# GpSimd instead of SyncE issues the loads of the values v in the recurrence of an RWKV-7 layer

## The reference

```
def step(state, inp):
    r_t, w_t, k_t, v_t, kk_t, a_t = inp
    sa = einsum('bhvk,bhk->bhv', state, kk_t)
    state = (state * w_t[:, :, None, :] - sa[..., None] * (kk_t * a_t)[:, :, None, :]
             + v_t[..., None] * k_t[:, :, None, :])
    return state, einsum('bhvk,bhk->bhv', state, r_t)
```

## Time and profile before

| | |
|---|---|
| three executions | 1603.55, 1608.61, 1597.57 us (median 1603.55) |
| profiled execution | 1597.2 us, its span 1595.4 us |
| busy share of the span | TensorE 91%, VectorE 32%, ScalarE 15%, GpSimd 12% |
| TensorE's granted clock over the span | 0.984 of full speed |
| recurrence | about 269 us (first fill of unit 0) to 537 us (first product of the next stage) |
| transfers issued by SyncE (queue q1) | 180192 packets, 479.31 MB, 78.4% of 16 engines |
| transfers issued by GpSimd (queue q0) | 5792 packets, 19.88 MB, 3.6% of 16 engines |
| four times eight `UV` loads | SyncE, 128 KB each, 5.2 us to landing (median) |

### The profile page before, as it was taken

How to read it: one execution, slowest core, us unless ns; L and a number is a source line. 1 busy time by engine, 2 the same in 40 slices (tenths; PEclk the granted TensorE clock), 3 DMA queues, 4 the chain that set the end, 5 groups by cost and what they waited for, 6 DMA issues and landing times.

```text
span 1595.4 us, 26196 instructions
## 1 busy us (share of the span) xinstructions
PE 1453.7 (91%) x11376; PEld 727.9 (46%) x11376; DVE 509.8 (32%) x712; ACT 239.9 (15%) x478; POOL 184.2 (12%) x349
## 2 busy tenths in 40 slices
PE   8999999988887895999989989989989989989977
PEld 6344455888887553434324324324324324324322
DVE  6666534666664564001101101101101101101103
ACT  3333321222212121100000000000000000000002
POOL 1323503433333210000000000000000000000000
PEclk9999999999999997899999999999999999999999
DMA  9245577766765635599999999999999999999994
GB/s 302 66 158 184 185 264 162 180 132 138 145 117 145 265 146 211 207 426 424 424 425 426 424 426 426 425 425 426 426 424 427 425 425 428 423 426 427 421 425 187
DMA packets 186071, 500.47 MB, mean 314 GB/s; under 512 B 125905, under 2 KB 135249, under 8 KB 153217
## 3 DMA queue, kind: packets, MB, share of 16 engines
q1 hardware_dynamic: 180192, 479.31, 78.4%
q0 software_dynamic: 5792, 19.88, 3.6%
HBM read 470.83 MB, written 28.33 MB: 313 GB/s over the span
## 4 chain that ended last, share of the span: by engine, by line
PE 32%; DMA 24%; DVE 2%; issue 1%; ACT 1%; DVEq 0%; SPq 0%
DMA ring<-in_exp_w_up 24%; PE pD L1555 14%; PE pG L1516 6%; PE pU L1536 6%; PE pX L1504 4%; PE pG L1536 3%; DVE res L1664 1%; DVE hid L1682 1%; PE pX L1543 1%; ACT hidT L1625 0%; DVE res L1700 0%; ACT xin L1608 0%; PE pX L1572 0%; ACT xin L1640 0%; ACT L1643 0%
## 5 line engine op out<-in xcount | busy, mean ns | idle before, releaser
L1682 DVE TENSOR_TENSOR hid<-silu,pU 128x512 f32<-128x512 f32 x32 | 20.6, 684 | 774.6 <-PE pU L1536 774.6
L1536 PE MATMUL pU<-ring,xin 128*64 128x512 f32 x768 | 173.8, 597 | 37.5 <-DMA ring<-in_exp_w_up 37.5
L1536 PE MATMUL pG<-ring,xin 128*64 128x512 f32 x768 | 171.3, 595 | 11.3 <-DMA ring<-in_exp_w_gate 10.7
L1555 PE MATMUL pD<-ring,hidT 128*64 128x512 f32 x768 | 167.9, 593 | 2.1 <-ACT hidT L1625 1.9
L1516 PE MATMUL pG<-yexp,scatter 128*128 128x512 f32 x256 | 124.4, 618 | 3.5 <-DVE res L1664 1.9
L1536 PEld LDWEIGHTS pU<-ring,xin 128*64 128x64 f32 x768 | 52.4, 137 | 157.4 <-issue 92.2
L1536 PEld LDWEIGHTS pG<-ring,xin 128*64 128x64 f32 x768 | 53.0, 137 | 116.7 <-issue 97.6
L1555 PEld LDWEIGHTS pD<-ring,hidT 128*64 128x64 f32 x768 | 55.4, 137 | 107.7 <-issue 107.0
L1664 DVE TENSOR_TENSOR res<-res,pG 128x512 f32<-128x512 f32 x128 | 87.0, 687 | 45.9 <-PE pG L1516 45.9
L1516 PEld LDWEIGHTS pG<-yexp,scatter 128*128 128x128 f32 x256 | 40.6, 188 | 87.1 <-DVE res L1664 62.9
L1504 PEld LDWEIGHTS pX<-pick,y 128*128 128x128 f32 x512 | 60.1, 197 | 5.4 <-issue 3.3
(11 more groups left out here) (238 smaller groups left out, 1732.3 us busy)
## 6 DMA issues: line engine op xcount, KB each, us to landing
ring<-in_exp_w_gate SPq DMA_DIRECT2D x48, 2048.0 KB, 34.6
ring<-in_exp_w_up SPq DMA_DIRECT2D x48, 2048.0 KB, 27.8
ring<-in_exp_w_down SPq DMA_DIRECT2D x48, 2048.0 KB, 28.8
lent_slot<-in_exp_w_up SPq DMA_DIRECT2D x16, 2048.0 KB, 20.5
lent_slot<-in_exp_w_gate SPq DMA_DIRECT2D x16, 2048.0 KB, 31.8
lent_slot<-in_exp_w_down SPq DMA_DIRECT2D x16, 2048.0 KB, 33.8
lent_slot<-in_rw_w_in SPq DMA_DIRECT2D x8, 1024.0 KB, 12.5
scratch_sw<-tok POOLq DMA_DIRECT2D x8, 512.0 KB, 3.9
```

Of the source, the lines that this page charges most:

```text
L1536: mm = pe.matmul(psum[f // 2][HEAD * s:HEAD * s + HEAD, :], xin[:, k, e, :], w[:, FF * r + HALF * f:FF * r + HALF * f + HALF], start=k == ...
L1555: mm = pe.matmul(pD[h][HEAD * s:HEAD * s + HEAD, :], hidT[:, j, c, HEAD * s:HEAD * s + HEAD], w[:, 4 * half + 2 * s + c % 2, HALF * h:HALF ...
L1682: dve.tensor_tensor(hid[:, j, :], silu[:, j, :], pU[j][:, :], ALU.mult).then_inc(hid_done, 1)
```

## The change

The four loads of each unit's values leave SyncE's queue and go into GpSimd's: that of unit 0 ahead of the first base inverse, that of unit n behind `base(n)`. The wait for y goes with them. The load of `v_last` goes to GpSimd as well, behind `base(7)` and `load_v(7)`. All waits guard the same buffers as before.

```diff
             blocks(0)
-            load_v(0)
             load_decays(2)
...
             for n in range(LAST):
-                if n:
-                    sp.wait_ge(y_mm, 2 * n)
-                load_v(n + 1)
                 if n + 3 < UNITS:
                     load_decays(n + 3)
...
             sp.wait_ge(tk_mm, 4 * LAST)
-            sp.dma_start(v_last, scr["v"][TILE_ORDER[0]]).then_inc(v_in[0], 16)
             sp.dma_start(keep["lnx_b"], io["rw_lnx_b"][0].partition_broadcast(P)).then_inc(keep["lnx_load"], 16)
...
+            def load_v(n):
+                if n >= 2:
+                    pool.wait_ge(y_mm, 2 * (n - 1))
+                if n < TILES:
+                    pool.wait_ge(v_out[tile(n)], 16)
+                for u in range(2):
+                    for e in range(2):
+                        src = scr["v"][tile(n)][rows(u), :].rearrange("t (c e v) -> t e c v", e=2, v=HEAD)[:, e]
+                        pool.dma_start(UV[n % 2][rows(1 - e), e, :, u, :], src).then_inc(v_in[n % 2], 16)
+
+            load_v(0)
             for n in range(UNITS):
                 base(n)
+                if n:
+                    load_v(n)
+            pool.wait_ge(tk_mm, 4 * LAST)
+            pool.dma_start(v_last, scr["v"][TILE_ORDER[0]]).then_inc(v_in[0], 16)
             pool.wait_ge(v_in[0], V_SUM * TILES + 16)
             add_bonus(pool, keep, 0, v_last)
```

More of the change, by code:

```diff
@@ L625, in load_keys @@
                     sp.dma_start(IN[:, s, :], src[n % 2, tile(n)].rearrange("p c s -> p (c s)")).then_inc(keys_in, 16)
[L627 to L633, removed]
             def blocks(n):
```

## The result

The changed kernel takes 1607.7 us (median of 20 executions, 1604.5 to 1611.8) against 1600.7 us for the kernel before (20 executions, 1596.6 to 1609.3). The medians differ by 7.0 us; the ratio by which all kernels are compared here is 1.0035, with a 95% interval of 1.0025 to 1.0046: +5.6 us (4.0 to 7.4), a small but certain loss. The profiled execution has a span of 1604.7 us, 9.3 us above that of before, so the two traces shown differ by more than the medians do. In the traces the first product behind the recurrence stands at 546.43 us instead of about 537 us, and from there to the end both need 1058 us: all of the difference arises ahead of that product, in the recurrence.

What follows compares the result with a forecast made beforehand. The recurrence's end bounds the kernel, its units released by TensorE or the inverses' round trip. 3 x 1.4 + 2.9 (unit 7, with `v_last`) less 1.0 for keys gives +6.1 us on 1601.7: 1608 us, range 1598 to 1620.

Steps and rivals of the forecast that it cites:

- SyncE's freed time is worth 0: SyncE's queue in the recurrence: 2.6 us of issues freed per unit, ahead of 10.5 us idling for the base: 0.
- GpSimd's issues, 0.75 us each, in time: Behind each base: four issues, 3.0 us, inside GpSimd's idle time; values land 2.0 to 3.6 us before use: cost 0.
- Late values: Rival: VectorE's work from SBUF holds GpSimd's issues, so TensorE waits for `UV`: 23 us with contention, 1625 us; chance 0.09.
- The traffic lengthens the trip, every other unit: `UV` packets meet the inverses' round trip (`XB` to scratch, `X`, `XT` back); delays pile up at units 1, 3, 5, 7.
- over 8 us at the start of unit 7: Sign of being right: TensorE waits for `XT` at units 1, 3, 5, 7, over 8 us in the last.
- Its size, d = 1.4 us: Growth of each inverses' round trip from 1.9 us of `UV` work, partly hidden: 1.4 us, between 0.8 and 2.2.
- the gaps: DMA engines are 0.77 busy over 3.25 us while `XB` is written, leaving 0.75 us that `UV` can fill.
- The rule that a DMA engine takes turns between queues: `UV` on its own queue would go ahead almost whole: 1.9 for 1.4 us four times, sum 2.0 us longer; not adopted.
- The base doesn't change: GpSimd's base inverse in each unit: assumed to run no slower, so no term in the sum.
- a slower base: Sign of being wrong altogether: the base inverse on GpSimd itself runs slower.
- v_last costs 1.5 us: GpSimd issues `v_last` during unit 7's inverse round trip; its 512 KB add 1.5 us there (0 to 1.5).
- The keys gain 1.0 us: Key loads ahead of `UV` in SyncE's queue land earlier, sparing VectorE's wait that reached TensorE: -1.0 us (0 to -4.7).

Runs made afterwards that it cites:

- the values alone: The change without the move of `v_last`, which stays in SyncE's queue, against the kernel before: 1.0041 (1.0026 to 1.0056), +6.6 us.

## Why the prediction was right, and where by luck

The forecast was +6.1 us (1608 us) and the outcome +5.6 by the ratio (+7.0 by the medians, 1607.7 us). By its steps:

- *SyncE's freed time is worth 0.* Shown: its wait for the base grew by 25.5 us in all (3.2 us per unit, where I had 2.6), and no kernel gained from it.
- *GpSimd's issues, 0.75 us each, in time.* 0.68 us each; no wait of TensorE for `UV`. Late values are refuted, and so is a stall of the issues by these products of VectorE: none of the 32 took over 0.72 us. In most units VectorE worked out of PSUM at those times, as I had said, but in unit 4 two products out of on-chip memory, like that of the earlier trace rows, ran over the first and the last issue. VectorE, then GpSimd's four issues in unit 4 and all 32 (shortest, median and longest ns):

```profile
398.89 1.22 DVE L1040 TENSOR_TENSOR BK<-lent_slot 64x1024 f32<-64x1024 f32 x1
...
401.06 1.22 DVE L1040 TENSOR_TENSOR BK<-lent_slot 64x1024 f32<-64x1024 f32 x1
```

```profile
398.92 2.73 POOL L732 DMA_DIRECT2D UV<-scratch_v  x4 [0.30 <-POOL XB L721]
...
L732 POOL DMA_DIRECT2D UV<-scratch_v x32: 683/683/718, 230.9 to 504.3; - x32
```

  With the values in the middle of the base, such products ran over the issues of five units, and the longest of the 32 was again 718 ns. The stall that the Trainium skill (SBUF — State Buffer, section SBUF: two separate sides) warns of for GpSimd's transfers is that under an operation of VectorE in a two-port mode, such as a 32-bit copy within on-chip memory. What ran here were products of two tensors, no such copies, so these issues don't contradict the warning, and no run here tests it.
- *The traffic lengthens the trip, every other unit.* That the traffic costs by where it meets the trip is shown by the place (ahead of the base +1.6 us, behind it +6.6, into the reads +13.4; ahead of and inside the base the trips stay as before) and by the amount (half of it costs 2.2 us at most); that delays pile up every other unit, by the values in the middle of the base. In the trace of the changed kernel, though, the trip of unit 5 did not grow (the other odd ones did); its start is late by what came before. Unit 5, which began without a wait, now waits 1.50 us. And I had expected TensorE to wait over 8 us at the start of unit 7; it waits 6.84, hardly more than before (6.67), because unit 6 ends later as well.
- *Its size, d = 1.4 us.* Near, and rather too small. `UV`'s work is 2.0 us (I took 1.9). With the values alone, the trips of units 1, 3, 6 and 7, for which TensorE already waited before, grew by 0.8, 2.3, 2.7 and 1.4 us, 1.8 in the mean. I had the gaps absorb the same share of every part; that half the values cost nothing measurable and all of them 6.6 us doesn't look so. The rule that a DMA engine takes turns between queues (the Trainium skill, DMA: Bandwidth & Descriptors, section Queues, rings and completion order), which I had valued 2.0 us higher and left out of the sum, agrees with the landing of the writes: 4.9 us with the values on a queue of their own, 4.1 us with them behind in the same one, a little later. With 1.9 us four times, less 1.0, it would give the values alone +6.6 us, as measured; but their interval, 4.2 to 9.0 us, also holds my +4.6, so the times don't decide it.
- *The base doesn't change.* Wrong by about 0.9 us per unit: bases 1 to 6 went from 15.35 to 16.25 us in the mean. I had named a slower base as a sign that would make the prediction wrong altogether; it came, and in unit 3 it counts for as much as the trip (2.1 and 2.3 us). No instruction was added to it; what differs is its phase against VectorE. GpSimd's issues are not the cause: with SyncE issuing the values between writes and reads, GpSimd issues nothing, and bases 1 to 6 take 16.4 us. No kernel isolates the phase, but the traces point to it: late units put VectorE's products of the queries on top of the base's start. In the changed kernel, GpSimd (first two instructions of base 3) and VectorE:

```profile
346.82 1.21 POOL L712 COPY XB<-con 128x256 f32<-128x256 f32 x1 [16.55 <-DMA NB<-scratch_blocks]
348.11 1.08 POOL L717 TENSOR_TENSOR step_sum<-NB,XB 128x15 f32<-128x15 f32 x1
```

```profile
346.55 2.55 DVE L1053 TENSOR_TENSOR QR<-lent_slot,decay 128x1024 f32<-128x1024 f32 x2
```

  Before, the same products were over before base 3 began at 346.69 us, and its first two instructions took 0.40 and 0.22 us:

```profile
343.41 2.35 DVE L1051 TENSOR_TENSOR QR<-lent_slot,decay 128x1024 f32<-128x1024 f32 x2
```

  In unit 7, for which VectorE prepares nothing, the base takes 11.8 us in every kernel here but the two that lengthen it on purpose. I had the row for this and used it for GpSimd's issues alone. It slowed the elementwise work and not the issues.
- *v_last costs 1.5 us.* It lengthens the last trip by 1.8 us, as the mechanism had it, but the kernel by nothing measurable (upper end of the interval +0.3 us). This term should have been 0.
- *The keys gain 1.0 us.* VectorE's three waits for `scratch_kd` are gone from the changed kernel's trace; that they bring 1 us isn't shown separately.

So the sum came out right in part by luck: two terms that by the traces were too small (trip and base: values alone +6.6, where my terms 4 x 1.4 - 1.0 gave +4.6) met one that was too large (`v_last`, 1.5). Two small misreadings changed nothing: I wrote that units take 30 to 38 us, while their starts in the trace of before lie 29.9 to 35.7 us apart; and I called the whole 11.65 us from the end of base 3 to unit 3 DMA, though SyncE's issues are part of it. Still open: how the 6.6 us divide between longer trips and slower bases, which pull each other along, and what in unit 7 gives 1.1 us back.

## What to carry to other kernels

A transfer moved to an idle engine's queue costs nothing there, but look at which transfers it will be in flight with: for the same 512 KB per unit one place cost about 1.6 us (with no change inside its interval), another 6.6, another 13.4. On a chain that skips a unit, each microsecond of delay counts at every other unit. Of the places tried here, the cheapest for the transfer was the old one, while the critical chain computes; moving it to where its issuing engine happened to be free cost time. And a late chain can also cost on the engine that computes it, if it slides under the work of another.

## What the runs showed of the hardware

- The same four issues take 2.7 us on GpSimd behind the base, 2.6 us in the median (2.6 to 3.8) on SyncE at the old place, and 3.8 to 4.7 us on SyncE right behind the `XB` writes.
- Elementwise work of GpSimd is stretched by VectorE's products that work from on-chip memory alone: single instructions from 0.3 to 1.2 us, a base from 11.8 (unit 7, without them) to 15.4 us. GpSimd's DMA issues, with such a product over them, stayed at 0.68 to 0.72 us.
- The 512 KB of values in 256-byte pieces took 2.0 us of all 16 DMA engines from GpSimd's queue.
